# Two-layer hybrid block on one core: who adds the gated part to the residual in the last passes of the closing stages

## The chip, the cores and the metric

One of the cores of a Trainium2 chip runs the whole program; the other cores are idle. The metric is the time of one execution on the device in microseconds (us). Everything is float32; the matrix products are split by hand into a high and a low part and summed over three products. The engines are named as the profile names them: PE is TensorE, DVE VectorE, ACT ScalarE, POOL GpSimd, SP the engine that issues DMAs here.

## The reference, cut to what matters

Two layers. In each, a token-mixing sublayer and a feed-forward sublayer each end with the same three steps: an output product, a gated residual sum, and a layer norm over the 1024 channels.

```python
x = _layernorm(alpha * x + mod[2] * lat_mix, ln1_g[i], ln1_b[i])
x = _layernorm(alpha * x + mod[5] * _conv_ffn(_modulate(x, mod[3], mod[4]), lp), ln2_g[i], ln2_b[i])
if not last:
    xc = _layernorm(alpha * xc + mod_c[2] * ctx_mix, ln1_g[i], ln1_b[i])
    xc = _layernorm(alpha * xc + mod_c[5] * _conv_ffn(_modulate(xc, mod_c[3], mod_c[4]), lp), ln2_g[i], ln2_b[i])
```

`x` has 512 latent tokens and `xc` 256 context tokens, which are dropped after the first layer's updates. `alpha` is `ALPHA`, the fourth root of 4.

## The kernel before

The program is a row of stages. At the end of each, all engines meet at a barrier, so a stage is as long as the engine that ends last in it. Tokens lie on the 128 partitions: `x` is [128, tiles, 1024], with six tiles of tokens in the first layer (`nt` = 6) and four in the second (`nt` = 4). Two stages of each layer update `x`: `close` (from 1.3 to 1.49 ms in the first layer, and from 3.12 to 3.27 ms in the second) and `ffn` (after it, to 2.10 ms and to the end). This case is about the end of these four.

**The output product.** TensorE makes, for each tile t and each half n of the 1024 output channels, a 128x512 block in a PSUM bank. In `close` there are two passes over all tiles, c = 0 and c = 1; the last is written tile by tile (`project(1, t, ...)`) so that VectorE can follow. In `ffn` the hidden channels come in chunks, with passes (chunk, n); for the last chunk (`LC`) the order of the blocks is the list `final`: (0,0), (1,0), (0,1), (1,1), (2,0), (3,0), (2,1), (3,1), and so on, in pairs (t, n). A tile is complete when its block with n = 1 is.

**What VectorE does with a block** (`projected` in `close`, `gated` in `ffn`), one after the other:

- the gate: `part = PSUM block * gate row` (L2084, L2391), which signals `z1`. `part` has two buffers, taken in turn
- the add: `x = ALPHA * x + part` in the first passes (L2086), `x = x + part` in the later ones of `ffn` (L2397), which signals `z2`
- in the last passes, the statistics of this half, `bn_stats` (L2088, L2400)

When a tile is complete, `moments(t)`: aggregate (L2092, L2404), add epsilon (L2094, L2406), and `(x - mean) * ln_g` over 1024 columns (L2095, L2407). ScalarE takes the square root (`root`, L2046, L2358). Then `scaled(t)`: a reciprocal of one column (L2099, L2411) and `x * rstd + ln_b` over 1024 columns (L2102, L2414). Then `next_stats(t)`, except in the last `ffn`: two `bn_stats` of the new `x` for the next stage's norm (L2107, L2419). VectorE's order is the written one; a semaphore is waited for wherever the next instruction reads what another, its own too, has written.

**GpSimd** makes in these stages the low parts of the weights, 128x1024 each (L2055, L2367), and in `ffn` those of the hidden activations (L2375). It has nothing else in `close` and `ffn`, and is idle once the last weights are split. **ScalarE** makes the high parts (L2018, L2330) and then only the roots. **SP** loads the weights, and in the last `ffn` stores each tile of `x` when `scaled` is done with it.

Elsewhere, in attention, GpSimd squares what VectorE has copied (L1519). Its code is of use below, because one instruction in several has a second wait:

```python
if j >= 2:
    pool.wait_ge(sem("ss"), j - 1)
for u in range(nq):
    pool.wait_ge(sem("o_read"), j * nq + u + 1)
    o = oq[:, j * nq + u, :]
    m = pool.tensor_tensor(sq[:, j % 2, u, :], o, o, ALU.mult)
```

## Time and profile before

| what | value |
|---|---|
| time, median of 3 runs | 3673.91 us (3664.45 to 3676.2) |
| the profiled execution | 3661.34 us, of which its span is 3659.4 us |
| mean granted TensorE clock in it | 0.976 |
| TensorE busy | 3373.4 us, 92% |
| VectorE busy | 1584.3 us, 43% |
| ScalarE busy | 1268.5 us, 35% |
| GpSimd busy | 1074.0 us, 29% |

Over the whole program TensorE is the busiest engine by far. At the end of the four stages in question it is not: it has made its last block and stands still while VectorE finishes the tiles, and the next stage can't begin before. So what counts here is VectorE's own chain of instructions, from the timeline of these stretches, and not the shares of the whole span.

### The profile page before, as it was taken

What the parts mean: (1) busy time and instruction counts of PE and PEld (TensorE: products, weight loads), DVE (VectorE), ACT (ScalarE), POOL (GpSimd) and SP (SyncE); (2) the same over time, 40 slices, a digit from 0 to 9 for tenths busy, and PEclk for the clock granted to TensorE, in tenths of its full rate; (3) what the DMA queues carried; (4) which work ended last, traced back from release to release, by engine and by line L of the source; (5) the groups of instructions that cost most, each with busy time, mean ns of one, the idle gap of its engine ahead of it and who ended that gap; (6) DMA issues with size and microseconds to landing.
All of it is one profiled execution on the core that took longest, in us unless ns stands there. A gap on an engine that the chain in (4) does not pass through costs nothing. (4 is left out here: it accounts for less than half of the span.)

```text
span 3659.4 us, 82761 instructions
## 1 busy us (share of the span) xinstructions
PE 3373.4 (92%) x36725; PEld 2692.7 (74%) x36725; DVE 1584.3 (43%) x2538; ACT 1268.5 (35%) x2184; POOL 1074.0 (29%) x645
## 2 busy tenths in 40 slices
PE   6989999999888999799999899999999898879998
PEld 4668887888655777687878676887778666568887
DVE  3243335442277646612112734445453476372224
ACT  3333233333365422321212143334444365233222
POOL 1111132233011512233333232223333114235453
PEclk9999999999999999899999999999999999999999
DMA  7664332342222333233332145334443313423332
GB/s 264 209 203 113 109 111 87 114 130 83 78 72 76 120 124 125 74 122 116 115 121 93 34 154 177 106 110 126 123 129 90 104 58 121 164 85 104 98 98 87
DMA packets 444861, 423.43 MB, mean 116 GB/s; under 512 B 15652, under 2 KB 372042, under 8 KB 437594
## 3 DMA queue, kind: packets, MB, share of 16 engines
q1 hardware_dynamic: 442922, 409.35, 35.7%
q10 hardware_dynamic: 1584, 8.78, 0.6%
q8 instruction: 291, 4.77, 0.6%
q14 instruction: 64, 0.52, 0.0%
HBM read 329.34 MB, written 88.74 MB: 114 GB/s over the span
## 5 line engine op out<-in xcount | busy, mean ns | idle before, releaser
L888 PE MATMUL ps<-I-322_h_hi,I-325_w_hi 128*128 128x256 f32 (+1 forms) x832 | 297.3, 357 | 4.5 <-PEq L124 4.5
L888 PE MATMUL ps<-I-323_h_lo,I-325_w_hi 128*128 128x256 f32 (+1 forms) x832 | 281.9, 339 | 0.0
L888 PE MATMUL ps<-I-322_h_hi,I-326_w_lo 128*128 128x256 f32 (+1 forms) x832 | 281.4, 338 | 0.0
L2367 POOL TENSOR_TENSOR I-18801_w_lo<-I-18799_w_raw,I-18800_w_hi 128x1024 fp32r<-128x1024 f32 x60 | 144.9, 2415 | 343.5 <-ACT I-18800_w_hi L2330 343.4
L888 PE MATMUL ps<-I-23551_h_hi,I-23554_w_hi 128*128 128x512 f32 (+1 forms) x544 | 211.9, 389 | 4.6 <-PEq L124 4.6
L888 PE MATMUL ps<-I-23552_h_lo,I-23554_w_hi 128*128 128x512 f32 (+1 forms) x544 | 199.9, 368 | 0.0
L888 PE MATMUL ps<-I-23551_h_hi,I-23555_w_lo 128*128 128x512 f32 (+1 forms) x544 | 199.9, 367 | 0.0
L2367 POOL TENSOR_TENSOR I-39041_w_lo<-I-39039_w_raw,I-39040_w_hi 128x1024 fp32r<-128x1024 f32 x60 | 144.4, 2407 | 154.6 <-ACT I-39040_w_hi L2330 154.6
L2330 ACT ACTIVATE I-18800_w_hi<-I-18799_w_raw 128x1024 fp32r<-128x1024 f32 x61 | 64.6, 1060 | 355.6 <-PE ps L365 235.9
L365 PE MATMUL ps<-I-18796_h_hi,I-18800_w_hi 128*128 128x512 f32 x704 | 183.0, 341 | 1.1 <-DVE I-18797_h_lo L402 1.1
L365 PE MATMUL ps<-I-18796_h_hi,I-18801_w_lo 128*128 128x512 f32 x704 | 181.7, 339 | 0.0
L365 PE MATMUL ps<-I-18797_h_lo,I-18800_w_hi 128*128 128x512 f32 x704 | 181.6, 339 | 0.0
L852 POOL TENSOR_TENSOR I-326_w_lo<-I-324_w_raw,I-325_w_hi 128x1024 fp32r<-128x1024 f32 x34 | 83.1, 2443 | 326.2 <-ACT I-325_w_hi L1132 326.2
L888 PEld LDWEIGHTS ps<-I-322_h_hi,I-325_w_hi 128*128 128x128 f32 x832 | 158.2, 190 | 25.6 <-issue 4.9
L888 PEld LDWEIGHTS ps<-I-322_h_hi,I-326_w_lo 128*128 128x128 f32 x832 | 158.4, 190 | 17.4
L888 PEld LDWEIGHTS ps<-I-323_h_lo,I-325_w_hi 128*128 128x128 f32 x832 | 158.8, 191 | 13.9
L1114 ACT ACTIVATE I-2000_result<-ps 128x512 f32<-128x512 f32 x104 | 51.3, 493 | 329.4 <-PE ps L888 329.3
L852 POOL TENSOR_TENSOR I-23555_w_lo<-I-23553_w_raw,I-23554_w_hi 128x1024 fp32r<-128x1024 f32 x34 | 84.6, 2487 | 269.5 <-ACT I-23554_w_hi L1132 269.5
L958 PE MATMUL ps<-I-49_x 64*64 64x32 f32 x3840 | 148.7, 219 | 1.4 <-issue 0.9
L365 PE MATMUL ps<-I-39036_h_hi,I-39040_w_hi 128*128 128x512 f32 x352 | 137.5, 391 | 1.8 <-DVE I-39037_h_lo L402 1.8
L365 PE MATMUL ps<-I-39036_h_hi,I-39041_w_lo 128*128 128x512 f32 x352 | 137.0, 389 | 0.0
L365 PE MATMUL ps<-I-39037_h_lo,I-39040_w_hi 128*128 128x512 f32 x352 | 137.0, 389 | 0.0
(902 smaller groups left out, 8752.0 us busy)
## 6 DMA issues: line engine op xcount, KB each, us to landing
I-324_w_raw<-in_w_in SPq DMA_DIRECT2D x67, 512.0 KB, 5.9
I-23553_w_raw<-in_w_in SPq DMA_DIRECT2D x67, 512.0 KB, 5.2
I-18809_ada_w<-in_ada_w SPq DMA_DIRECT2D x24, 1024.0 KB, 6.0
I-18799_w_raw<-in_ffn_up SPq DMA_DIRECT2D x44, 512.0 KB, 3.9
I-39039_w_raw<-in_ffn_up SPq DMA_DIRECT2D x44, 512.0 KB, 3.9
proj_d<-I-2000_result SPq DMA_DIRECT2D x52, 384.0 KB, 3.1
I-508_ada_w<-in_ada_w SPq DMA_DIRECT2D x16, 1024.0 KB, 5.6
I-18799_w_raw<-in_ffn_down SPq DMA_DIRECT2D x22, 512.0 KB, 3.4
```

What stands on the lines that cost most here:

```text
L365: m = pe.matmul(dst[:, at:at + n], w[wi][:, k, :], a[ai][:, k, at:at + n], start=k == 0 and i == 0, stop=k == kt - 1 and i == 2)
L852: pool.tensor_tensor(lo(s), raw(s), hi(s).bitcast(F32), ALU.subtract).then_inc(sem("w_lo"), 1)
L888: m = pe.matmul(bank(6 + i % 2, n_c), w[:, k, :], hv[:, k, c0:c0 + n_c], start=k == 0 and v == 0, stop=k == KT - 1 and v == 2)
L958: return pe.matmul(side(ps[rows(i), (2 + d) * 512 + c0:(2 + d) * 512 + c0 + C], n_lv, 1 - d), Y[d][rows(i), c0:c0 + C], side(TT[d][rows(i) ...
L1114: act.activation(res[:, s % 2, c0:c0 + n_c], bank(6 + i % 2, n_c), ACT.Copy, scale=DH_A ** -0.5 if J_Q <= slots[s][0] < J_K else 1.0).then ...
L2330: act.activation(pair(g)[0], rings[0][:, g % 3, :, :], ACT.Copy).then_inc(sem("w_hi"), 1)
L2367: pool.tensor_tensor(pair(g)[1], rings[0][:, g % 3, :, :], pair(g)[0].bitcast(F32), ALU.subtract).then_inc(sem("w_lo"), 1)
```

## The change

In the last passes, all adds but the very last one of each stage move from VectorE to GpSimd. GpSimd gets a loop behind its weight splits: wait for the block's `z1` (the gate's product is in `part`), and for the add before it (`z2`), then `x = x + part` in place, signalling `z2`. In `close` that add had the factor `ALPHA` in it, which GpSimd's instruction doesn't; ScalarE multiplies the second half of every tile by `ALPHA` beforehand, in place, as soon as `x` is back in SBUF (semaphore `xa`).

VectorE's order in the last passes changes too. After the gate of block i it runs `scaled` and `next_stats` of the tile completed before (the "tile in front"), where there is one, and only then the statistics of block i, which need GpSimd's add; `moments` of the tile follows at once. The last tile's `scaled` and `next_stats` come behind the loop. In `close`, each block after the first has a tile in front. In `ffn`, a block has one only if the block before it in `final` has n = 1: (1,1), (2,0), (3,1) and (4,0) of twelve blocks in the first layer, (1,1) and (2,0) of eight in the second, beside the last block. The last block of a stage, whose add VectorE keeps, has one too.

```diff
--- before.py
+++ after.py
@@ -2045,6 +2045,9 @@
                         act.wait_ge(sem("var"), t + 1)
                         act.activation(rs[:, t:t + 1], rs[:, t:t + 1], ACT.Sqrt).then_inc(sem("std"), 1)
 
+                    act.wait_ge(sem("x_back"), 16)
+                    for t in range(nt):
+                        act.activation(x[:, t, 512:1024], x[:, t, 512:1024], ACT.Copy, scale=ALPHA).then_inc(sem("xa"), 1)
                     for t in range(nt):
                         root(t)
 
@@ -2054,6 +2057,12 @@
                         pool.wait_ge(sem("w_hi"), n - 1)
                         pool.tensor_tensor(lo(n)[:, 0:kt_of(n), :], raw(n)[:, 0:kt_of(n), :], hi(n)[:, 0:kt_of(n), :].bitcast(F32),
                                            ALU.subtract).then_inc(sem("w_lo"), 1)
+                    for t in range(nt - 1):
+                        i, xt = nt + t, x[:, t, 512:1024]
+                        pool.wait_ge(sem("xa"), t + 1)
+                        pool.wait_ge(sem("z1"), i + 1)
+                        pool.wait_ge(sem("z2"), i)
+                        pool.tensor_tensor(xt, xt, part[:, i % 2, :], ALU.add).then_inc(sem("z2"), 1)
 
                 @block.vector
                 def _(dve):
@@ -2082,8 +2091,19 @@
                         if i >= 2:
                             dve.wait_ge(sem("z2"), i - 1)
                         dve.tensor_tensor(part[:, i % 2, :], o_of(c, t), gate[:, t // LT, cols], ALU.mult).then_inc(sem("z1"), 1)
-                        dve.wait_ge(sem("z1"), i + 1)
-                        dve.scalar_tensor_tensor(x[:, t, cols], x[:, t, cols], ALPHA, part[:, i % 2, :], ALU.mult, ALU.add).then_inc(sem("z2"), 1)
+                        if c == 0 or t == nt - 1:
+                            dve.wait_ge(sem("z1"), i + 1)
+                            dve.wait_ge(sem("z2"), i)
+                            if c:
+                                dve.wait_ge(sem("xa"), nt)
+                                dve.tensor_tensor(x[:, t, cols], x[:, t, cols], part[:, i % 2, :], ALU.add).then_inc(sem("z2"), 1)
+                            else:
+                                dve.scalar_tensor_tensor(x[:, t, cols], x[:, t, cols], ALPHA, part[:, i % 2, :], ALU.mult, ALU.add).then_inc(sem("z2"), 1)
+                        if c == 0:
+                            moved(c, t)
+
+                    def moved(c, t):
+                        i, cols = c * nt + t, slice(c * 512, (c + 1) * 512)
                         dve.wait_ge(sem("z2"), i + 1)
                         dve.bn_stats(st[:, t, c, :], x[:, t, cols]).then_inc(sem("st"), 1)
 
@@ -2142,9 +2162,13 @@
                     dve.wait_ge(sem("ln_b"), 16)
                     for t in range(nt):
                         projected(1, t)
+                        if t:
+                            scaled(t - 1)
+                            next_stats(t - 1)
+                        moved(1, t)
                         moments(t)
-                        scaled(t)
-                        next_stats(t)
+                    scaled(nt - 1)
+                    next_stats(nt - 1)
 
         def ffn(l, h, last):
 
@@ -2374,6 +2398,11 @@
                             pool.wait_ge(sem("hf_hi"), j + 1)
                             pool.tensor_tensor(hp[1][:, j % CH, :], cv[:, j % 2, 0:n_tok], hp[0][:, j % CH, :].bitcast(F32),
                                                ALU.subtract).then_inc(sem("hf_lo"), 1)
+                    for t, n in final[:-1]:
+                        i, xt = 2 * LC * nt + final.index((t, n)), x[:, t, n * 512:(n + 1) * 512]
+                        pool.wait_ge(sem("z1"), i + 1)
+                        pool.wait_ge(sem("z2"), i)
+                        pool.tensor_tensor(xt, xt, part[:, i % 2, :], ALU.add).then_inc(sem("z2"), 1)
 
                 @block.vector
                 def _(dve):
@@ -2389,15 +2418,19 @@
                         if i >= 2:
                             dve.wait_ge(sem("z2"), i - 1)
                         dve.tensor_tensor(part[:, i % 2, :], pt_of(cn, t), gate[:, t // LT, c], ALU.mult).then_inc(sem("z1"), 1)
+                        if cn[0] == LC and (t, cn[1]) != final[-1]:
+                            return
                         dve.wait_ge(sem("z1"), i + 1)
+                        dve.wait_ge(sem("z2"), i)
                         if cn[0] == 0:
                             dve.scalar_tensor_tensor(x[:, t, c], x[:, t, c], ALPHA, part[:, i % 2, :], ALU.mult, ALU.add).then_inc(sem("z2"), 1)
                         else:
                             dve.wait_ge(sem("z2"), pass_no(cn) * nt + t + 1 - 2 * nt)
                             dve.tensor_tensor(x[:, t, c], x[:, t, c], part[:, i % 2, :], ALU.add).then_inc(sem("z2"), 1)
-                        if cn[0] == LC:
-                            dve.wait_ge(sem("z2"), i + 1)
-                            dve.bn_stats(st[:, t, cn[1], :], x[:, t, c]).then_inc(sem("st"), 1)
+
+                    def moved(t, n):
+                        dve.wait_ge(sem("z2"), 2 * LC * nt + final.index((t, n)) + 1)
+                        dve.bn_stats(st[:, t, n, :], x[:, t, n * 512:(n + 1) * 512]).then_inc(sem("st"), 1)
 
                     def moments(t):
                         dve.wait_ge(sem("st"), 4 * (t // 2) + 3 + t % 2)
@@ -2451,13 +2484,19 @@
                             ada_add(dve, sem, u, l + 1, u, 7)
                     dve.wait_ge(sem("ln_g"), 16)
                     dve.wait_ge(sem("ln_b"), 16)
-                    for t, n in final:
+                    def finished(t):
+                        scaled(t)
+                        if not last:
+                            next_stats(t)
+
+                    for i, (t, n) in enumerate(final):
                         gated((LC, n), t)
+                        if i and final[i - 1][1]:
+                            finished(final[i - 1][0])
+                        moved(t, n)
                         if n:
                             moments(t)
-                            scaled(t)
-                            if not last:
-                                next_stats(t)
+                    finished(final[-1][0])
 
         for l in range(DEPTH):
             last = l == DEPTH - 1
```

VectorE, `close` of the first layer, from `moments(0)` to `moments(1)`. Before:

```order
L2095 SCALAR_TENSOR_TENSOR I-49_x<-I-49_x,I-17270_mean_var,I-17267_ln_g 128x1024
L2099 RECIPROCAL I-17271_rstd<-I-17271_rstd 128x1
L2102 SCALAR_TENSOR_TENSOR I-49_x<-I-49_x,I-17271_rstd,I-17268_ln_b 128x1024
L2107 BN_STATS I-67_x_stats<-I-49_x 128x6 x2
L2084 TENSOR_TENSOR I-17265_part<-ps,I-17266_gate_row 128x512
L2086 SCALAR_TENSOR_TENSOR I-49_x<-I-49_x,I-17265_part 128x512
L2088 BN_STATS I-17269_stats<-I-49_x 128x6
L2092 BN_AGGR I-17270_mean_var<-I-17269_stats 128x2
L2094 TENSOR_SCALAR I-17271_rstd<-I-17270_mean_var 128x1
```

After:

```order
L2115 SCALAR_TENSOR_TENSOR I-49_x<-I-49_x,I-17270_mean_var,I-17267_ln_g 128x1024
L2093 TENSOR_TENSOR I-17265_part<-ps,I-17266_gate_row 128x512
L2119 RECIPROCAL I-17271_rstd<-I-17271_rstd 128x1
L2122 SCALAR_TENSOR_TENSOR I-49_x<-I-49_x,I-17271_rstd,I-17268_ln_b 128x1024
L2127 BN_STATS I-67_x_stats<-I-49_x 128x6 x2
L2108 BN_STATS I-17269_stats<-I-49_x 128x6
L2112 BN_AGGR I-17270_mean_var<-I-17269_stats 128x2
L2114 TENSOR_SCALAR I-17271_rstd<-I-17270_mean_var 128x1
```

The gate of tile 1 has moved in front of tile 0's reciprocal, and VectorE's add between the gate and the statistics is gone.

GpSimd, end of the first `close`, with the semaphores that each instruction waits for, in the order of the listing (a semaphore has the name of an earlier stage that had the same number: I-856 is `z2`, I-162 `z1` and I-247 `xa`). In the same listing the squares of attention (L1519) with two waits have `o_read` first and `ss` last. Before:

```order
L2055 TENSOR_TENSOR I-13893_w_lo<-I-13891_w_raw,I-13892_w_hi 128x512 [waits I-174_columns] x14
L2055 TENSOR_TENSOR I-13893_w_lo<-I-13891_w_raw,I-13892_w_hi 128x1024 [waits I-174_columns] x4
L2055 TENSOR_TENSOR I-17273_of_lo<-I-13891_w_raw,I-17272_of_hi 128x1024 [waits I-174_columns] x3
L2055 TENSOR_TENSOR I-13893_w_lo<-I-13891_w_raw,I-13892_w_hi 128x1024 [waits I-174_columns]
L119 UNCONDITIONAL_BRANCH
L123 ISA [waits barrier_Pool_Activation_PE_DVE_SP_gather]
```

After:

```order
L2058 TENSOR_TENSOR I-13893_w_lo<-I-13891_w_raw,I-13892_w_hi 128x512 [waits I-174_columns] x14
L2058 TENSOR_TENSOR I-13893_w_lo<-I-13891_w_raw,I-13892_w_hi 128x1024 [waits I-174_columns] x4
L2058 TENSOR_TENSOR I-17273_of_lo<-I-13891_w_raw,I-17272_of_hi 128x1024 [waits I-174_columns] x3
L2058 TENSOR_TENSOR I-13893_w_lo<-I-13891_w_raw,I-13892_w_hi 128x1024 [waits I-174_columns]
L2065 TENSOR_TENSOR I-49_x<-I-49_x,I-17265_part 128x512 [waits I-856_w_act,I-162_dots,I-247_ada_add] x5
L119 UNCONDITIONAL_BRANCH
L123 ISA [waits barrier_Pool_Activation_PE_DVE_SP_gather]
```

Behind the weight splits stand five adds, each with three waits, of which `z1` is the second. In `ffn` an add has two waits, listed as `z2` and then `z1`, which is last.

VectorE, last `ffn`, from the gate of block (2,0) to the gate of (2,1). Before:

```order
L2391 TENSOR_TENSOR I-39047_part<-ps,I-39048_gate_row 128x512
L2397 TENSOR_TENSOR I-49_x<-I-49_x,I-39047_part 128x512
L2400 BN_STATS I-39049_stats_out<-I-49_x 128x6
L2391 TENSOR_TENSOR I-39047_part<-ps,I-39048_gate_row 128x512
L2397 TENSOR_TENSOR I-49_x<-I-49_x,I-39047_part 128x512
L2400 BN_STATS I-39049_stats_out<-I-49_x 128x6
L2391 TENSOR_TENSOR I-39047_part<-ps,I-39048_gate_row 128x512
L2397 TENSOR_TENSOR I-49_x<-I-49_x,I-39047_part 128x512
L2400 BN_STATS I-39049_stats_out<-I-49_x 128x6
```

After:

```order
L2420 TENSOR_TENSOR I-39116_part<-ps,I-39117_gate_row 128x512
L2444 RECIPROCAL I-39120_rstd_out<-I-39120_rstd_out 128x1
L2447 SCALAR_TENSOR_TENSOR I-49_x<-I-49_x,I-39120_rstd_out,I-39122_ln_b 128x1024
L2433 BN_STATS I-39118_stats_out<-I-49_x 128x6
L2420 TENSOR_TENSOR I-39116_part<-ps,I-39117_gate_row 128x512
L2433 BN_STATS I-39118_stats_out<-I-49_x 128x6
L2420 TENSOR_TENSOR I-39116_part<-ps,I-39117_gate_row 128x512
L2433 BN_STATS I-39118_stats_out<-I-49_x 128x6
L2437 BN_AGGR I-39119_mean_var_out<-I-39118_stats_out 128x2
```

Tile 1's `scaled` stands between the gate and the statistics of (2,0); between gate and statistics of (3,0) there is nothing.

## Rows read from the trace of the kernel before

**Rows 1.** Stretches: from:to, us; busy PE, PEld, DVE, ACT, POOL; PEclk; DMA

```profile
1448.30:1486.80 38.50, 26.13 (x115) 21.12 (x113) 37.22 (x61) 1.22 (x6) 0.00 (x0) 0.87 0.00 0
2045.60:2100.30 54.70, 44.70 (x198) 36.68 (x196) 51.71 (x78) 3.56 (x8) 5.53 (x3) 0.95 0.02 7
```

**Rows 2.** Timeline (start, us, engine, line, operation, tiles): VectorE, a tile of close

```profile
1454.76 0.67 DVE L2084 TENSOR_TENSOR I-17265_part<-ps,I-17266_gate_row 128x512 f32<-128x512 f32 x1
1455.47 0.69 DVE L2086 SCALAR_TENSOR_TENSOR I-49_x<-I-49_x,I-17265_part 128x512 f32<-128x512 f32 x1
1456.19 0.69 DVE L2088 BATCH_NORM_STATS2 I-17269_stats<-I-49_x 128x6 f32<-128x512 f32 x1
...
1457.24 1.27 DVE L2095 SCALAR_TENSOR_TENSOR I-49_x<-I-49_x,I-17270_mean_var,I-17267_ln_g 128x1024 f32<-128x1024 f32 x1
1458.43 0.16 DVE L2099 RECIPROCAL I-17271_rstd<-I-17271_rstd 128x1 f32<-128x1 f32 x1
1458.62 1.28 DVE L2102 SCALAR_TENSOR_TENSOR I-49_x<-I-49_x,I-17271_rstd,I-17268_ln_b 128x1024 f32<-128x1024 f32 x1
1459.94 1.29 DVE L2107 BATCH_NORM_STATS2 I-67_x_stats<-I-49_x 128x6 f32<-128x512 f32 x2
1461.15 0.67 DVE L2084 TENSOR_TENSOR I-17265_part<-ps,I-17266_gate_row 128x512 f32<-128x512 f32 x1
```

**Rows 3.** Timeline: VectorE, end of the last ffn

```profile
3645.46 0.69 DVE L2391 TENSOR_TENSOR I-39047_part<-ps,I-39048_gate_row 128x512 f32<-128x512 f32 x1 [1.93 <-PE ps L2320]
...
3654.41 1.28 DVE L2414 SCALAR_TENSOR_TENSOR I-49_x<-I-49_x,I-39051_rstd_out,I-39053_ln_b 128x1024 f32<-128x1024 f32 x1
```

**Rows 4.** Timeline: GpSimd and VectorE at once, first passes of close in layer 1

```profile
3237.56 2.86 POOL L2055 TENSOR_TENSOR I-35367_w_lo<-I-35365_w_raw,I-35366_w_hi 128x1024 fp32r<-128x1024 f32 x1
...
3238.19 0.69 DVE L2088 BATCH_NORM_STATS2 I-37911_stats<-I-49_x 128x6 f32<-128x512 f32 x1
...
3241.67 2.39 POOL L2055 TENSOR_TENSOR I-35367_w_lo<-I-35365_w_raw,I-35366_w_hi 128x1024 fp32r<-128x1024 f32 x1 [1.25 <-ACT I-35366_w_hi L2018]
...
3242.32 2.29 DVE L2086 SCALAR_TENSOR_TENSOR I-49_x<-I-49_x,I-37907_part 128x512 f32<-128x512 f32 x1
```

**Rows 5.** Timeline: two pairs of GpSimd and VectorE that start almost together

```profile
1405.16 2.40 POOL L2055 TENSOR_TENSOR I-13893_w_lo<-I-13891_w_raw,I-13892_w_hi 128x1024 fp32r<-128x1024 f32 x1 [3.46 <-ACT I-13892_w_hi L2018]
...
1405.21 3.17 DVE L2124 TENSOR_TENSOR I-13890_y<-I-13890_y,I-17264_gated 128x768 f32<-128x768 f32 x1
...
2555.72 1.85 POOL L848 TENSOR_TENSOR I-23555_w_lo<-I-23553_w_raw,I-23554_w_hi 128x512 fp32r<-128x512 f32 x1 [6.95 <-ACT I-23554_w_hi L1130]
...
2555.74 0.69 DVE L1229 TENSOR_TENSOR I-24933_Bh<-I-24931_a,I-24929_EN 128x512 f32<-128x512 f32 x1
```

**Rows 6.** Timeline: VectorE releases GpSimd, at two places of attention

```profile
1002.35 0.29 DVE L1551 COPY I-49_x<-ps 128x128 f32<-128x128 f32 x1 [0.97 <-PE ps L1457]
...
1002.72 0.40 POOL L1519 TENSOR_TENSOR I-13908_o_sq<-I-49_x 128x128 f32<-128x128 f32 x1 [2.93 <-DVE I-49_x L1551]
...
1040.77 0.29 DVE L1551 COPY I-49_x<-ps 128x128 f32<-128x128 f32 x1 [0.61 <-PE ps L1457]
...
1041.21 0.40 POOL L1519 TENSOR_TENSOR I-13908_o_sq<-I-49_x 128x128 f32<-128x128 f32 x1 [4.07 <-DVE I-49_x L1551]
```

**Rows 7.** Line L864, ns min/median/max: in-place adds on GpSimd

```profile
L864 POOL TENSOR_TENSOR I-66_ada_row<-I-66_ada_row,I-2000_result x8: 1259/1288/1619, 477.9 to 897.3; 128x512 f32<-128x512 f32 x8
```

**Rows 8.** Timeline: the first ffn as its last chunk opens, GpSimd and VectorE

```profile
2048.28 2.85 POOL L2367 TENSOR_TENSOR I-18797_h_lo<-I-18799_w_raw,I-18796_h_hi 128x1024 fp32r<-128x1024 f32 x1
...
2055.07 0.69 DVE L2400 BATCH_NORM_STATS2 I-18810_stats_out<-I-49_x 128x6 f32<-128x512 f32 x1
```

**Rows 9.** Timeline: ScalarE around the last passes of the first close

```profile
1441.60 1.06 ACT L2018 ACTIVATE I-13892_w_hi<-I-13891_w_raw 128x1024 fp32r<-128x1024 f32 x1 [8.86 <-PE ps L1962]
1442.67 1.28 ACT L2046 ACT_TABLE_LOAD   x1
...
1450.96 0.20 ACT L2046 ACTIVATE I-17271_rstd<-I-17271_rstd 128x1 f32<-128x1 f32 x1 [7.01 <-DVE I-17271_rstd L2094]
```

## The prediction

> **What bounds the kernel now.** I read the table of stretches first, for the ends of the four stages [rows 1]. In the last passes of the first `close` VectorE is busy for 37.22 of 38.50 us and in those of the first `ffn` for 51.71 of 54.70, TensorE for 26.13 and 44.70: TensorE is ahead, and the stage ends with VectorE. Then the timeline of VectorE [rows 2]. One tile of `close` takes from 1454.76 to 1461.15, 6.39 us, with no gap longer than a semaphore. The last `ffn` is the exception: before the gate of (2,1) VectorE waits 1.93 us for TensorE [rows 3]. What is lost before that point costs only what exceeds 1.93; from there on all of it counts, since the last `x * rstd + ln_b` ends at 3655.69 and its store closes the program. So the change is worth what it does to VectorE's chain, four times, and it hangs on three things: what an add costs on GpSimd, whether something covers it, and which engine gets in first where both want to read two SBUF tiles.
>
> **Two engines at once.** [rows 4] and [rows 5] show what overlap does. VectorE's add at 3242.32 takes 2.29 us, not 0.69, and ends 0.55 after GpSimd's split (3244.61 against 3244.06): it had to wait for the whole GpSimd instruction and lost 0.14 less than its length. The statistics at 3238.19, with one SBUF input, take 0.69 with GpSimd at work. So gates (one input in PSUM) and statistics run beside a GpSimd add; `(x - mean) * ln_g` and `x * rstd + ln_b` do not. The other way round GpSimd waits: at 2555.74 VectorE has its 0.69 us although it starts 0.02 after GpSimd, whose split takes 1.85 and ends 1.14 after VectorE's end. At 1405.21, 0.05 behind GpSimd, VectorE waits (3.17 us). The border lies between 0.02 and 0.05 us.
>
> **An add that nothing covers.** GpSimd's in-place add of 128x512 takes 1.29 us in the median, 1.26 to 1.62 [rows 7]; I take 1.29. The handover from VectorE to GpSimd takes 0.08 us with one wait (1002.64 to 1002.72) and 0.15 where the late semaphore is listed before another (1041.06 to 1041.21) [rows 6]. The adds of `ffn` have `z1` last, so 0.08; those of `close` have it in the middle, so 0.15. Back to VectorE I take 0.07. From the gate's end to the statistics are now 0.08 + 1.29 + 0.07 = 1.44 us in `ffn` and 1.51 in `close`; before, 1456.19 - 1455.43 = 0.76 [rows 2]. A bare add costs **0.68** or **0.75 us**.
>
> **An add with a tile in front.** Let the gate end at T. The reciprocal starts 0.08 before T and `x * rstd + ln_b` 0.19 after that, at T + 0.11 (as 1458.51, 1458.43 and 1458.62 in [rows 2]).
> In `close` GpSimd comes at T + 0.15, after VectorE: VectorE runs to T + 1.39, GpSimd ends 1.14 later, at T + 2.53, and the two statistics for the next stage run meanwhile, to T + 2.72. The block's own statistics start at T + 2.64, when the add has just landed (2.60): nothing is lost. The tile is shorter by the add (0.72) and by 0.12, since the reciprocal no longer waits behind a dependent instruction: **-0.84 us**, 5.55 for 6.39.
> In `ffn` GpSimd comes at T + 0.08, 0.03 to 0.04 before VectorE. That is inside the border of [rows 5]; it is nearer to the 0.05 that lost, so I let GpSimd win. It ends at T + 1.37 and VectorE 1.28 - 0.14 = 1.14 later, at T + 2.51 for T + 1.39. The 1.12 us are more than the 0.84: **+0.28 us**.
>
> What a blocked GpSimd add costs after VectorE's end is 1.14 here. The Trainium skill (SBUF — State Buffer, "A bandwidth-pool intuition that's wrong (but worth ruling out)") gives for descriptor work of GpSimd "blocked until DVE-end + ~115 ns". By it the add would end at T + 2.80, 0.27 later than by the row, the statistics would wait about 0.23, and the six covered tiles of `close` would make the sum 1.4 us larger; I go by the row.
>
> **The four stages.**
> - First `close`: adds of tiles 0 to 4 moved, tile 0 bare, four covered; tile 5 keeps its add but gains the 0.12: 0.75 - 4 x 0.84 - 0.12 = **-2.7**.
> - Second `close`: 0.75 - 2 x 0.84 - 0.12 = **-1.1**.
> - First `ffn`. At its opening GpSimd still splits weights. The last split, 2.85 us from 2048.28 [rows 8], is 0.45 shorter once VectorE no longer cuts in: it ends at 2050.68, and only then comes the add of (0,0), which on VectorE slipped in between two splits. Add to 2051.97, statistics 2052.04, gate of (1,0) 0.61 later, to 2053.33, statistics 2054.77, gate of (0,1) to 2056.06, statistics 2057.50, where they were at 2055.07: +2.4. Then four covered (+1.1), four bare ((3,0), (2,1), (5,0), (4,1): +2.7), and -0.12: **+6.1**.
> - Last `ffn`: the same opening +2.4, covered (1,1) and (2,0) +0.6, bare (3,0) +0.7, together 3.7, of which 1.93 go into the wait for TensorE [rows 3]: +1.8. Bare (2,1) +0.7, -0.1: between 2.1 and 2.4, **+2.2**.
>
> ScalarE's six multiplications by `ALPHA` cost nothing: 128x1024 takes it 1.06 us and it is idle for 7.01 from 1443.95 on [rows 9]; even at 1.06 each they and the table load end by 1450.4, before the first root at 1450.96, and the first, wanted at 1449.1, by 1443.8. Without that cover the first GpSimd add would wait. VectorE's additional waits on `z2` are met before they are asked. TensorE's banks are freed by the gates, which in `close` come earlier; in the first `ffn` they come up to 2 us later, and TensorE is several us ahead. VectorE has nothing queued behind the new wait for GpSimd that could run meanwhile, which is why a bare add costs its full length.
>
> The sum is -2.7 - 1.1 + 6.1 + 2.2 = **+4.5 us**, on a profiled execution of 3661.34 (span 3659.4): 3665.8. That execution lies 12.6 below the median, 3673.91, so against the median I say **3678.4**.
>
> **Rivals.**
> - GpSimd first everywhere. The order in `close` rests on a difference of 0.04 us. For it: the handover in `close` is taken from one place with two waits, not three. Against: [rows 6] has the same listing. Then each of the six covered tiles costs +0.28 and not -0.84, and a bare one 0.68: +1.7 and +1.1 for the two `close`, in all +11.1, 3685.0.
> The Trainium skill (SBUF — State Buffer, "Who interferes with whom") has it that "Issue order, not op shape, decides who blocks"; that rule gives either outcome.
> - VectorE first everywhere, as the 0.02 of [rows 5] allows. The covered blocks of the first `ffn` then gain 0.84: +1.6. In the last there are no statistics for a next stage to cover the rest of the add (T + 2.60 against T + 2.43), so it becomes +2.6. In all +0.4 to +1, 3674.6.
> - The slower one: GpSimd's add is long. [rows 7] has 1.62 beside 1.29. If that is its price on `x`, and GpSimd goes first, all 26 adds (5 + 3 + 11 + 7) stand in VectorE's chain with 0.33 more each: 11.1 + 8.6 = +19.7, 3693.6. With GpSimd first, any add over 1.29 carries the sum over 11 us, which is 0.3%. Against: the median of eight is 1.288, and the maximum looks like one that waited for VectorE.
> - The faster one: no lock between these instructions. The covered blocks gain everywhere, and the sum is about -2, 3672. Against it stand [rows 4, 5].
>
> **How the numbers follow.** The forecast has 0.47, VectorE first 0.22, GpSimd first 0.19, the long add 0.08, no lock 0.04. A measurement of this kernel can tell about 0.3%, 11 us, from no change. Of the forecast and its neighbours nearly all lies within it; of GpSimd first about half, since 11.1 is on the border. Slower by over 0.3%: 0.08 + 0.09 = 0.17. Faster by over 0.3% comes from no case, only from the spread of runs: 0.04. Within: 0.79. For the range I add to the cases the spread of the runs, 3664.45 to 3676.2: 3664 to 3688 leaves out the long add and little else.
>
> **What would show it.** Right: in `close`, tiles 1 to 4 at 5.55 us each, `x * rstd + ln_b` at 1.28 us, GpSimd adds recorded as about 2.4 us because they wait; in `ffn`, `x * rstd + ln_b` of covered blocks at about 2.4 us beside GpSimd adds of 1.29; bare blocks with 1.4 to 1.5 us from the gate's end to the statistics; the first `ffn` some 6 us longer, the last 2. Wrong: the durations exchanged between the two engines; bare adds well over 1.3; GpSimd's first add of `ffn` not behind the splits; or another part of the program that moves by more than the four ends, as the TensorE clock after them could.

## The result, and the profile of the changed kernel

The changed kernel takes **3682.17 us** (median of 13 executions, 3673.85 to 3689.55), the kernel before 3670.26 (13, 3664.45 to 3676.2). The ratio is **1.0034**, with a 95% interval from 1.0024 to 1.0043: slower by 12.5 us (8.8 to 15.8). The profiled execution of the changed kernel has a span of 3677.2 us. Of the experiments below, e5 had two executions out of eleven that took 4281 and 4287 us at a granted clock of 0.74; they are left out of its ratio.

Most of what follows is measured by four **ends**: from the first gate of the last passes to the first aggregate of the next stage's norm, and in the last `ffn` to the end of the span. The kernel before has 39.43, 55.59, 26.58 and 38.27 us in program order. The changed kernel has 41.32, 61.01, 27.69 and 40.08: +1.89, +5.42, +1.11, +1.81, together **+10.24 us**. The two spans differ by 17.8; 7.0 of that are there before the first changed place (its gate is at 1455.37 for 1448.37), where the two programs do the same work. Executions of one kernel differ by as much, so I go by the ends, and for the whole by the ratio.

The profile of the changed kernel, its head and then the two stretches that answer to [rows 1] (from:to, us; busy PE, PEld, DVE, ACT, POOL; PEclk; DMA):

```profile
span 3677.2 us, 82811 instructions
...
PE 3381.7 (92%) x36725; PEld 2699.5 (73%) x36725; DVE 1572.0 (43%) x2512; ACT 1272.8 (35%) x2194; POOL 1105.7 (30%) x671
```

```profile
1455.30:1495.50 40.20, 26.11 (x115) 21.10 (x113) 37.75 (x56) 1.22 (x6) 6.45 (x5) 0.85 0.00 0
2052.40:2112.20 59.80, 44.71 (x198) 36.69 (x196) 44.92 (x67) 3.56 (x8) 19.13 (x14) 0.91 0.02 6
```

In the first `close` VectorE has five instructions less, but its busy time has not fallen (37.75 for 37.22): what remains takes longer. In the first `ffn` it is busy 6.8 us less than before, in a stretch that is 5.1 longer: it stands idle.

VectorE, first `close`, from the gate of tile 0 to that of tile 2, as in [rows 2] (start, us, engine, line, operation, tiles):

```profile
1455.37 0.67 DVE L2093 TENSOR_TENSOR I-17265_part<-ps,I-17266_gate_row 128x512 f32<-128x512 f32 x1
1457.50 0.69 DVE L2108 BATCH_NORM_STATS2 I-17269_stats<-I-49_x 128x6 f32<-128x512 f32 x1 [1.46 <-POOL I-49_x L2065]
...
1459.74 0.68 DVE L2093 TENSOR_TENSOR I-17265_part<-ps,I-17266_gate_row 128x512 f32<-128x512 f32 x1
1460.34 0.15 DVE L2119 RECIPROCAL I-17271_rstd<-I-17271_rstd 128x1 f32<-128x1 f32 x1
1460.53 2.41 DVE L2122 SCALAR_TENSOR_TENSOR I-49_x<-I-49_x,I-17271_rstd,I-17268_ln_b 128x1024 f32<-128x1024 f32 x1
1462.97 1.29 DVE L2127 BATCH_NORM_STATS2 I-67_x_stats<-I-49_x 128x6 f32<-128x512 f32 x2
1464.17 0.68 DVE L2108 BATCH_NORM_STATS2 I-17269_stats<-I-49_x 128x6 f32<-128x512 f32 x1
...
1466.39 0.69 DVE L2093 TENSOR_TENSOR I-17265_part<-ps,I-17266_gate_row 128x512 f32<-128x512 f32 x1
```

GpSimd in the same stretch:

```profile
1456.18 1.29 POOL L2065 TENSOR_TENSOR I-49_x<-I-49_x,I-17265_part 128x512 f32<-128x512 f32 x1 [4.05 <-DVE I-17265_part L2093]
1460.56 1.30 POOL L2065 TENSOR_TENSOR I-49_x<-I-49_x,I-17265_part 128x512 f32<-128x512 f32 x1 [3.09 <-DVE I-17265_part L2093]
```

`x * rstd + ln_b` takes 2.41 us for the 1.28 of [rows 2], and GpSimd's add has its 1.30: GpSimd holds the way to SBUF and VectorE waits, although the record has GpSimd start 0.03 us *behind* VectorE. A tile takes 6.65 us (1459.74 to 1466.39) where it took 6.39. All four covered adds of the first `close` and both of the second read like this.

The first `ffn`: VectorE in the opening, with the statistics of (0,0) and the gate and statistics of (0,1), and `x * rstd + ln_b` under the first covered add, that of (1,1); then GpSimd in the same stretch:

```profile
2058.76 0.69 DVE L2433 BATCH_NORM_STATS2 I-18836_stats_out<-I-49_x 128x6 f32<-128x512 f32 x1 [5.62 <-POOL I-49_x L2405]
...
2062.05 0.67 DVE L2420 TENSOR_TENSOR I-18833_part<-ps,I-18834_gate_row 128x512 f32<-128x512 f32 x1
2064.12 0.69 DVE L2433 BATCH_NORM_STATS2 I-18836_stats_out<-I-49_x 128x6 f32<-128x512 f32 x1 [1.40 <-POOL I-49_x L2405]
...
2067.14 2.33 DVE L2447 SCALAR_TENSOR_TENSOR I-49_x<-I-49_x,I-18838_rstd_out,I-18840_ln_b 128x1024 f32<-128x1024 f32 x1
```

```profile
2049.40 8.08 POOL L2391 TENSOR_TENSOR I-18823_h_lo<-I-18825_w_raw,I-18822_h_hi 128x1024 fp32r<-128x1024 f32 x3
2057.45 1.28 POOL L2405 TENSOR_TENSOR I-49_x<-I-49_x,I-18833_part 128x512 f32<-128x512 f32 x1
...
2062.80 1.28 POOL L2405 TENSOR_TENSOR I-49_x<-I-49_x,I-18833_part 128x512 f32<-128x512 f32 x1 [1.40 <-DVE I-18833_part L2420]
2067.11 1.28 POOL L2405 TENSOR_TENSOR I-49_x<-I-49_x,I-18833_part 128x512 f32<-128x512 f32 x1 [3.03 <-DVE I-18833_part L2420]
```

Here GpSimd starts 0.03 ahead and wins, as forecast. The first add begins only behind the third weight split, so that VectorE waits 5.62 us, and a bare add keeps it idle for 1.40 us.

### The profile page after: what moved, and what is told of

Its sections match the earlier page's. It is cut to its first block and busy times, and to the rows that moved or that the text cites. A ratio compares the mean times of both kernels' runs of the same rounds, so it can differ in the third digit from the quotient of the medians.

```text
span 3677.2 us, 82811 instructions
## 1 busy us (share of the span) xinstructions
PE 3381.7 (92%) x36725; PEld 2699.5 (73%) x36725; DVE 1572.0 (43%) x2512; ACT 1272.8 (35%) x2194; POOL 1105.7 (30%) x671
## 5 line engine op out<-in xcount | busy, mean ns | idle before, releaser
L2391 POOL TENSOR_TENSOR I-18827_w_lo<-I-18825_w_raw,I-18826_w_hi 128x1024 fp32r<-128x1024 f32 x60 | 145.2, 2421 | 342.2 <-ACT I-18826_w_hi L2354 342.0
L888 PE MATMUL ps<-I-23602_h_hi,I-23605_w_hi 128*128 128x512 f32 (+1 forms) x544 | 212.2, 390 | 4.6 <-PEq L124 4.6
L888 PE MATMUL ps<-I-23603_h_lo,I-23605_w_hi 128*128 128x512 f32 (+1 forms) x544 | 200.2, 368 | 0.0
L888 PE MATMUL ps<-I-23602_h_hi,I-23606_w_lo 128*128 128x512 f32 (+1 forms) x544 | 200.2, 368 | 0.0
L2391 POOL TENSOR_TENSOR I-39110_w_lo<-I-39108_w_raw,I-39109_w_hi 128x1024 fp32r<-128x1024 f32 x60 | 144.3, 2406 | 154.8 <-ACT I-39109_w_hi L2354 154.8
L365 PE MATMUL ps<-I-18822_h_hi,I-18826_w_hi 128*128 128x512 f32 x704 | 183.0, 341 | 1.1 <-DVE I-18823_h_lo L402 1.1
L365 PE MATMUL ps<-I-18822_h_hi,I-18827_w_lo 128*128 128x512 f32 x704 | 182.0, 340 | 0.0
L365 PE MATMUL ps<-I-18823_h_lo,I-18826_w_hi 128*128 128x512 f32 x704 | 180.0, 337 | 0.0
L888 PEld LDWEIGHTS ps<-I-322_h_hi,I-326_w_lo 128*128 128x128 f32 x832 | 159.3, 191 | 17.8
L365 PE MATMUL ps<-I-39105_h_hi,I-39109_w_hi 128*128 128x512 f32 x352 | 137.6, 391 | 1.8 <-DVE I-39106_h_lo L402 1.8
L365 PE MATMUL ps<-I-39105_h_hi,I-39110_w_lo 128*128 128x512 f32 x352 | 137.0, 389 | 0.0
```

The source lines that it names most:

```text
L365: m = pe.matmul(dst[:, at:at + n], w[wi][:, k, :], a[ai][:, k, at:at + n], start=k == 0 and i == 0, stop=k == kt - 1 and i == 2)
L888: m = pe.matmul(bank(6 + i % 2, n_c), w[:, k, :], hv[:, k, c0:c0 + n_c], start=k == 0 and v == 0, stop=k == KT - 1 and v == 2)
L2391: pool.tensor_tensor(pair(g)[1], rings[0][:, g % 3, :, :], pair(g)[0].bitcast(F32), ALU.subtract).then_inc(sem("w_lo"), 1)
```

## The experiments

| kernel | four ends, against before | sum | ratio to before (95%) |
|---|---|---|---|
| changed kernel | +1.89, +5.42, +1.11, +1.81 | +10.24 | 1.0034 (1.0024 to 1.0043) |
| e1_vector_first | -2.56, +1.27, -1.13, +2.22 | -0.21 | 0.9999 (0.9987 to 1.0012) |
| e2_close_alone | +1.89, +0.01, +1.12, +0.02 | +3.05 | 1.0015 (1.0006 to 1.0025) |
| e3_order_alone | -0.17, -0.24, +0.17, +0.30 | +0.06 | 1.0004 (0.9994 to 1.0014) |
| e4_covered_vector_first | -3.12, -0.81, -1.45, +0.30 | -5.08 | 0.9983 (0.9973 to 0.9992) |
| e5_last_block_old_order | -3.12, -1.07, -1.44, 0.00 | -5.64 | 0.9980 (0.9970 to 0.9991) |
| e6_one_wait_more | -2.59, +5.66, -1.15, +1.88 | +3.80 | 1.0006 (0.9995 to 1.0018) |
| e7_opening_back | +1.88, +3.88, +1.11, +0.51 | +7.38 | not timed |
| e8_two_waits_more | -2.57, +1.27, -0.84, +2.17 | +0.03 | 0.9997 (0.9986 to 1.0008) |
| e9_e5_again | -3.13, -1.09, -1.46, -0.01 | -5.69 | 0.9979 (0.9967 to 0.9990) |

Each ratio is against executions of the kernel before on the same occasion. The ratios follow the sums: times 3670, they are +12.5, -0.4, +5.5, +1.5, -6.2, -7.3, +2.2, -1.1 and -7.7 us, and the interval of each holds its sum.

**e1: GpSimd made to come second.** Each covered add also waits for the reciprocal of the tile in front, behind which VectorE's `x * rstd + ln_b` stands.

```diff
+                        if t:
+                            pool.wait_ge(sem("rstd"), t)
...
+                        e = final.index((t, n))
+                        if e and final[e - 1][1]:
+                            pool.wait_ge(sem("rstd"), final[e - 1][0] + 1)
```

> The changed kernel, but every GpSimd add that has a tile in front also waits for the reciprocal of that tile, so that it starts some 0.1 us after VectorE's x * rstd + ln_b instead of within 0.04 us of it. Theory (the loss in the covered blocks is the shared read path, taken by the engine that asks first, and GpSimd asked first in both stages): VectorE's x * rstd + ln_b goes from about 2.4 us back to 1.28, the GpSimd adds are recorded at about 2.3, a tile of close takes 5.55 us for 6.64 of the changed kernel, the covered blocks of the first ffn 1.1 us less each. The four ends together: +0.6 us against the kernel before, where the changed kernel had +10.2; ratio about 1.000. Rival (GpSimd has precedence whoever asks first, or the slow x * rstd + ln_b has another reason): the instruction stays at 2.4 us, each covered tile gets another 0.1 us longer, the ends stay at +10 to +11.

VectorE's and GpSimd's rows of the first covered pair:

```profile
1460.91 1.28 DVE L2124 SCALAR_TENSOR_TENSOR I-49_x<-I-49_x,I-17271_rstd,I-17268_ln_b 128x1024 f32<-128x1024 f32 x1
```

```profile
1461.05 2.30 POOL L2067 TENSOR_TENSOR I-49_x<-I-49_x,I-17265_part 128x512 f32<-128x512 f32 x1 [3.20 <-DVE I-17271_rstd L2121]
```

The durations have changed engines: 1.28 and 2.30. The tile of `close` takes 5.53 us, for the 5.55 that I had worked out for this order. The order of the two engines at twelve places is worth 10.4 us, as much as the whole slowdown. Against the numbers of the rival "VectorE first everywhere", the two `ffn` come to +1.27 and +2.22 for +1.6 and +2.6.

**e2: the change in `close` alone**, both `ffn` as before.

```diff
-                    for t, n in final[:-1]:
-                        i, xt = 2 * LC * nt + final.index((t, n)), x[:, t, n * 512:(n + 1) * 512]
-                        pool.wait_ge(sem("z1"), i + 1)
-                        pool.wait_ge(sem("z2"), i)
-                        pool.tensor_tensor(xt, xt, part[:, i % 2, :], ALU.add).then_inc(sem("z2"), 1)
...
-                            finished(final[i - 1][0])
```

> Only the two close stages are changed, both ffn are those of the kernel before. Theory (the loss is made of bare adds and of lost races, block by block): the closes keep +1.9 and +1.1 us, the ffn stages are as before, together +3.0 us, ratio 1.001. Rival (the changed kernel's time comes mainly from outside the four ends, where its profiled execution was 7 us later before the first of them began): the ratio stays at 1.002 or more though the ffn stages are as before.

The ends add: the stages do not act on each other. TensorE's clock in the stretches behind them, which the prediction named as a possible second effect, doesn't show in them: the unchanged stages stay within 0.02 us.

**e3: VectorE's new order alone.** All adds stay on VectorE; it finishes the tile in front behind the next gate, and makes the add and the statistics after that. In `moved` of both stages stands (here that of `ffn`)

```diff
+                        dve.wait_ge(sem("z1"), i + 1)
+                        dve.tensor_tensor(x[:, t, c], x[:, t, c], part[:, i % 2, :], ALU.add).then_inc(sem("z2"), 1)
```

(in `close` the add is the one with `ALPHA`, as before), and GpSimd's loops and ScalarE's multiplications are gone.

> VectorE's new order (gate of the next block, then reciprocal, x * rstd + ln_b and statistics of the tile in front, then the block's own add and statistics) with all adds still on VectorE; nothing on GpSimd, no multiplication on ScalarE. Theory: the order gains 0.12 us for each block with a tile in front, since two dependent instructions no longer stand next to each other, 16 blocks in all: the ends together -1.6 to -1.9 us; nothing waits for GpSimd, x * rstd + ln_b takes 1.28 us everywhere. Rival (the order itself costs something, as through ScalarE's root coming late or stores going out late): the ends at or above zero.

This missed. A tile of `close` does gain 0.12 (6.27 for 6.39), but VectorE now asks for the gate before it finishes the tile in front, and may have to wait for a bank that TensorE hasn't filled, in `close` and in the first `ffn`:

```profile
1458.78 0.69 DVE L2084 TENSOR_TENSOR I-17265_part<-ps,I-17266_gate_row 128x512 f32<-128x512 f32 x1 [0.39 <-PE ps L1962]
...
2062.02 0.69 DVE L2400 TENSOR_TENSOR I-18807_part<-ps,I-18808_gate_row 128x512 f32<-128x512 f32 x1 [0.31 <-PE ps L2329]
```

Before, the work on the tile in front filled these waits. In the last `ffn` the gain falls into waits for TensorE, and what the old order had done there now stands behind the last gate.

**e4: only covered adds on GpSimd, and VectorE first.** As e1, but VectorE keeps the add of tile 0 in `close`, the eight uncovered blocks of the first `ffn`, and all of the last `ffn`.

```diff
-                    for t in range(nt - 1):
+                    for t in range(1, nt - 1):
...
+            given = [] if last else [b for a, b in zip(final, final[1:]) if a[1] and b != final[-1]]
-                    for t, n in final[:-1]:
+                    for t, n in given:
```

> Only the adds that have a tile in front and next-stage statistics to hide under are on GpSimd (four in the first close, two in the second, four in the first ffn, none in the last), with the wait for the reciprocal as in e1; the bare ones are back on VectorE. Theory: -0.84 us for each of the ten and -0.12 for the last block of each stage: -3.5, -1.8, -3.5 and -0.1, together -8.9 us, ratio 0.9976, faster than both kernels. Rival (precedence of GpSimd): +0.3 us for each of the ten, together +3 us, ratio 1.001.

The two `close` come 0.4 us short of what was expected (-3.12 for -3.5, -1.45 for -1.8): the gate of tile 1 waits 0.40 and 0.30 us for TensorE there, as in e3. The first `ffn` is far short: -0.81 for -3.5. There the eleven intervals from gate to gate add up to 44.7 us, 4.06 each, and four of them are 4.08, which is what TensorE takes for a block. So TensorE sets the pace of the gates now, and VectorE waits for it:

```profile
2087.27 0.69 DVE L2426 TENSOR_TENSOR I-18837_part<-ps,I-18838_gate_row 128x512 f32<-128x512 f32 x1 [0.66 <-PE ps L2347]
...
2091.35 0.69 DVE L2426 TENSOR_TENSOR I-18837_part<-ps,I-18838_gate_row 128x512 f32<-128x512 f32 x1 [0.31 <-PE ps L2347]
...
2092.88 1.28 DVE L2453 SCALAR_TENSOR_TENSOR I-49_x<-I-49_x,I-18842_rstd_out,I-18844_ln_b 128x1024 f32<-128x1024 f32 x1
2094.19 1.29 DVE L2458 BATCH_NORM_STATS2 I-67_x_stats<-I-49_x 128x6 f32<-128x512 f32 x2
```

Before the gates of this stretch VectorE waits 3.45 us for TensorE in all, where it waited 1.22 before: 2.2 of the missing 2.7 us. The last gate comes 3.4 us earlier against the first than before (44.7 for 48.1), but tile 4's last two steps now stand behind it, and the rest of the stage is 10.08 us long for 7.47.

**e5: the old order where GpSimd has no add.** As e4, but VectorE finishes the tile in front ahead of the gate for the last block of the first `ffn` and in all of the last `ffn`.

```diff
                     for i, (t, n) in enumerate(final):
+                        if i and final[i - 1][1] and (t, n) not in given:
+                            finished(final[i - 1][0])
                         gated((LC, n), t)
-                        if i and final[i - 1][1]:
+                        if i and final[i - 1][1] and (t, n) in given:
                             finished(final[i - 1][0])
```

> As e4_covered_vector_first, with one edit: VectorE finishes the tile in front (scaled, and next_stats where there is one) before the gate, as the kernel before does, for the last block of the first ffn and for all blocks of the last ffn; only where GpSimd has the add (the two close stages, and the covered blocks of the first ffn) it is finished behind the gate. Theory A (e4's shortfall in the first ffn is that TensorE's blocks, 4.08 us apart, set its gates, so that work put behind the last gate, which comes when TensorE has made its block, only makes the tail longer): the first ffn improves from -0.81 to about -1.1, the last ffn from +0.30 to 0.0, the two close stay at -3.1 and -1.45; sum -5.7 for e4's -5.08. Theory B (the shortfall is a cost of the GpSimd add in these blocks, not of the order): both ffn stages stay as in e4, sum -5.1. Against the kernel before the ratio would be about 0.998 by either.

As by the first theory: -1.07 and 0.00. The order at these blocks is worth 0.26 and 0.30 us. The rest of e4's shortfall stays, as do the intervals between the gates up to the last but one, and VectorE still waits 3.18 us for TensorE: it is TensorE's pace, with 44.7 us of work in a stretch that was 48.1.

**e9: e5 once more.**

> The kernel of e5_last_block_old_order once more on another occasion, because two of its eleven executions took 4281 and 4287 us at a mean granted clock of 0.74, with nothing else unusual. Theory A (a disturbance from outside the kernel): no such execution here, ends of the four stages as in e5 within 0.1 us (-3.1, -1.1, -1.4, 0.0), ratio to the kernel before between 0.997 and 0.999. Theory B (the kernel's order of work brings the clock down now and then): about one execution in five again over 4200 us at a clock of about 0.74.

None of its twelve executions took more than 3675.29 us, which speaks for theory A; what disturbed the two isn't known. The ends repeat within 0.02 us. This kernel is **faster than the kernel before**, by 0.2%, and so than the changed one, whose ratio is 1.0034.

**e6 and e8: waits that order nothing.** Each covered GpSimd add of the changed kernel gets one more wait (e6), in `ffn` a second one (e8), for things made microseconds earlier.

```diff
+                        if t:
+                            pool.wait_ge(sem("mv"), t)
...
+                        e = final.index((t, n))
+                        if e and final[e - 1][1]:
+                            pool.wait_ge(sem("mv"), final[e - 1][0] + 1)
+                            pool.wait_ge(sem("st"), 4 * (final[e - 1][0] // 2) + 3 + final[e - 1][0] % 2)
```

The last line is e8's alone.

> The changed kernel with one more wait in front of each covered GpSimd add, on the aggregate of the tile in front, which is made some microseconds earlier, so that the wait is met before it is asked. It orders nothing; it can only make GpSimd's instruction start a few hundredths of a microsecond later. Theory A (whoever starts first by some border holds both engines' way to SBUF; in the changed kernel GpSimd starts 0.033 us behind VectorE in close and still wins, the border is 0.033 to 0.044): in close the GpSimd add starts 0.05 to 0.1 later, VectorE wins, tiles go from 6.64 to 5.53 and the two close stages from +1.9 and +1.1 to about -2.6 and -1.1; in ffn GpSimd starts at most 0.04 behind VectorE and still wins, tiles stay at 6.58, +5.4 and +1.8; sum about +3.5. If the additional wait costs more there (0.06 or more behind VectorE), ffn's covered tiles go to 5.53 too and the sum is about -0.2. Theory B (what e1 changed was the order given by the added dependence and its length of over 0.1 us, and a few hundredths decide nothing): tiles stay at 6.64 and 6.58, sum +10.2.

> As e6_one_wait_more, with a second wait that is met before it is asked (on the statistics of the tile in front) before each covered GpSimd add of the two ffn stages; in the listing z1, the late one, then stands first with three behind it, as in close in e6, where that put GpSimd's start 0.124 to 0.131 us behind VectorE's. Theory A (whoever starts first holds the way to SBUF, and waits listed behind the late one delay the start by about 0.05 us each): in ffn too GpSimd starts 0.12 to 0.13 behind VectorE and VectorE wins; covered tiles go from 6.64 to 5.53; the four ends are those of e1_vector_first, -2.6, +1.3, -1.1 and +2.2, sum -0.2 against the kernel before and -10.4 against the changed kernel; the ratio to before is 1.000, where the changed kernel's was 1.0034. Theory B (in ffn e1's dependence on the reciprocal was needed, a mere delay isn't enough): ffn stays as in e6, +5.7 and +1.9, sum +3.8, ratio 1.001.

e6, VectorE and then GpSimd, a covered pair of the first `close` and one of the first `ffn`:

```profile
1458.74 1.28 DVE L2124 SCALAR_TENSOR_TENSOR I-49_x<-I-49_x,I-17271_rstd,I-17268_ln_b 128x1024 f32<-128x1024 f32 x1
...
2061.63 2.40 DVE L2452 SCALAR_TENSOR_TENSOR I-49_x<-I-49_x,I-18842_rstd_out,I-18844_ln_b 128x1024 f32<-128x1024 f32 x1
```

```profile
1458.87 2.30 POOL L2067 TENSOR_TENSOR I-49_x<-I-49_x,I-17265_part 128x512 f32<-128x512 f32 x1 [3.19 <-DVE I-17265_part L2095]
...
2061.66 1.29 POOL L2410 TENSOR_TENSOR I-49_x<-I-49_x,I-18837_part 128x512 f32<-128x512 f32 x1 [3.09 <-DVE I-18837_part L2425]
```

e8, the same pair of `ffn`:

```profile
2063.45 1.29 DVE L2453 SCALAR_TENSOR_TENSOR I-49_x<-I-49_x,I-18842_rstd_out,I-18844_ln_b 128x1024 f32<-128x1024 f32 x1
```

```profile
2063.57 2.32 POOL L2411 TENSOR_TENSOR I-49_x<-I-49_x,I-18837_part 128x512 f32<-128x512 f32 x1 [3.19 <-DVE I-18837_part L2426]
```

In `close` the one wait puts GpSimd's start from 0.03 to 0.13 us behind VectorE's, and VectorE wins: 5.53 us for a tile. In `ffn` it puts it from 0.03 ahead to 0.03 behind, and GpSimd still wins; with the second it is 0.13 behind and VectorE wins. A delay of GpSimd by 0.10 to 0.15 us at twelve places takes 10.2 us off the changed kernel. The end of e8's second `close` is 0.3 us short of the forecast: VectorE stands 1.24 us at the barrier there, where it is 0.95 in e6.

**e7: the opening of `ffn` on VectorE again**, the adds of (0,0) and (1,0).

```diff
-                    for t, n in final[:-1]:
+                    for t, n in final[2:-1]:
...
-                        if cn[0] == LC and (t, cn[1]) != final[-1]:
+                        if cn[0] == LC and (t, cn[1]) in final[2:-1]:
```

> The changed kernel with the adds of the first two blocks of each ffn's last passes, (0,0) and (1,0), on VectorE again; GpSimd's adds begin with (0,1). Theory A (the opening costs about 2.2 us in the first ffn because GpSimd's first add waits behind its last weight split, and then two adds stand bare): the first ffn goes from +5.4 to about +3.9 (two bare adds at 0.68 gone, and the wait for the split gone or hidden), the last ffn from +1.8 to about +0.5; the close stages stay at +1.9 and +1.1; sum about +7.4. Theory B (the opening's loss is a wait of VectorE for TensorE or weights that the adds have nothing to do with): the sum stays at +10.2.

As expected, +3.88 and +0.51. These two adds cost the changed kernel 1.54 us in the first `ffn` and 1.30 in the last. What is left of the +2.2 at the statistics of (0,1) is 0.7, the bare add of that block.

## Why the prediction was right in its range and wrong in its mechanism

The predicted time, 3678.4 us, is 3.8 below what was measured, and the range holds it. The difference to the kernel before was forecast as +4.5; it is +10.2 by the ends and +12.5 by the ratio, just over the 0.3% that the forecast took as the bound of "same". That is the rival "GpSimd first everywhere", +11.1, to which I gave 0.19. The miss lies in the two `close`: +1.9 and +1.1 where -2.7 and -1.1 were forecast; the two `ffn` came 0.7 and 0.4 below their forecast. The time fits better than the difference by luck: the median of three runs that it starts from, 3673.91, lies 3.65 above that of the thirteen, 3670.26.

- **The step that failed** is "In `close` GpSimd comes at T + 0.15, after VectorE: VectorE runs". It takes 0.04 us behind VectorE for a safe distance, because the border had been read from [rows 5] as "between 0.02 and 0.05 us" with GpSimd ahead. In all six covered tiles of `close` GpSimd was recorded 0.027 to 0.035 us behind, and it won. The 0.02 of [rows 5] isn't a start against an idle engine. The instruction in front of it, in the trace of before:

```profile
2555.13 0.68 DVE L1227 TENSOR_TENSOR I-24943_kk_in<-I-24943_kk_in,I-24937_Lx 128x512 f32<-128x512 f32 x1
```

  also reads two SBUF tiles, and VectorE follows straight on. And the same pair stands in every trace of this case. In the changed kernel's, 0.02 us apart as well, it comes out the other way:

```profile
2566.64 1.29 POOL L848 TENSOR_TENSOR I-23606_w_lo<-I-23604_w_raw,I-23605_w_hi 128x512 fp32r<-128x512 f32 x1 [6.95 <-ACT I-23605_w_hi L1130]
```

```profile
2566.66 1.81 DVE L1229 TENSOR_TENSOR I-24984_Bh<-I-24982_a,I-24980_EN 128x512 f32<-128x512 f32 x1
```

  VectorE waits there and in seven other traces; it wins in before, e7 and e9. So 0.02 ahead was itself the border, and one for a VectorE that follows straight on. Where VectorE has finished what stood in front of it, and that read PSUM or one SBUF tile, as in the covered tiles, the border is another, and the trace of before has pairs on its far side that the prediction didn't use. Here VectorE is 0.05 ahead, with the gate's input in PSUM in front of it, and wins:

```profile
3126.13 0.69 DVE L2124 TENSOR_TENSOR I-35364_y<-I-35364_y,I-37906_gated 128x512 f32<-128x512 f32 x1
...
3126.18 1.78 POOL L2055 TENSOR_TENSOR I-35367_w_lo<-I-35365_w_raw,I-35366_w_hi 128x512 fp32r<-128x512 f32 x1 [9.50 <-ACT I-35366_w_hi L2018]
```

  Before has eight such pairs, with GpSimd 0.044 to 0.052 behind, all like this. Over the eleven traces, GpSimd won 25 of 26 such pairs when it was recorded 0.018 to 0.035 behind (the one that it lost is in e4, at 0.032) and none of 89 at 0.038 to 0.056. So by recorded starts this border lies between 0.03 and 0.04 us behind VectorE.
- **The starts were right to 0.01 us**, and that 0.01 counted: GpSimd at T + 0.14 (forecast 0.15) and VectorE at T + 0.11 in `close`; T + 0.08 and T + 0.11 in `ffn`. At the 0.04 that the forecast had in `close`, VectorE would probably have won after all; the rows of before couldn't decide it, and the rival said that the order rests on this difference. What each order costs was right as well: a tile of `close` takes 5.53 with VectorE first (5.55), 6.65 with GpSimd first (6.39 + 0.28). The first `close` came out at 0.70 (the bare tile) + 4 x 0.255 - 0.12 + 0.29, where 0.29 is the barrier: VectorE stands there for 1.31 us, for 1.02 before. The prediction has no term for it. The second is 0.70 + 2 x 0.27 - 0.12.
- **Bare adds**: 0.70 us in `close` (0.75 forecast), 0.64 in `ffn` (0.68; 2.68 for 2.04 from gate to gate). The 1.29 of [rows 7] is right, so the long add falls.
- **Covered adds of `ffn`**: +0.19 (6.58 for 6.39), forecast +0.28. The forecast let VectorE end 1.14 after GpSimd's end; it is 1.08.
- **The opening**: +2.2 (the statistics of (0,1) at 2064.12, 11.7 us after the first gate), forecast 2.4. Thus the first `ffn` is 2.2 + 4 x 0.64 + 4 x 0.19 - 0.12 = 5.4 for 6.1, and the last 1.81 for 2.2.
- **ScalarE's multiplications** cost nothing, as forecast: six in 3.22 us from 1449.54, and the root's table is loaded by 1454.05, 4.61 us before the first root.

Of the two rules of the Trainium skill in the prediction, "Issue order, not op shape, decides who blocks" (SBUF — State Buffer, "Who interferes with whom") leaves out that GpSimd may be recorded up to 0.035 us later and still be the one that blocks. The other, "blocked until DVE-end + ~115 ns" (the Trainium skill, the same page, "A bandwidth-pool intuition that's wrong (but worth ruling out)"), which is measured there on descriptor work, is not what an add shows: the whole of it ends 1.15 us after VectorE, which is 0.14 less than its own 1.29.

## What to carry to other kernels

When work moves to an engine that shares a way to memory with the first, work out which of the two comes first at that moment, and make the order certain by a dependence rather than by some hundredths of a microsecond: here that decided between +10 and 0 us. Move only what something covers (a bare add lost 0.64 to 0.70 us each time), and keep the work on the tile in front ahead of a wait that may be long, since behind it the wait is idle. And ask how far the other engine is behind: where TensorE had 44.7 us of work in 48.1, four covered adds gained 1.1 us and not 3.5.

## What the runs showed of the hardware

- Where both engines read two SBUF tiles and VectorE has finished what stood in front (which read PSUM or one SBUF tile), GpSimd wins also when it is recorded 0.026 to 0.035 us later (the covered pairs of `close` in the changed kernel, e2 and e7 and of `ffn` in e6, 24 in all); it lost one pair at 0.032 (e4), one at 0.038 (e2), eight at 0.044 to 0.052 (before), and all covered pairs at 0.124 to 0.140 (e1, e4, e5, e8, e9 and the `close` of e6).
- Where VectorE follows straight on another instruction that reads two SBUF tiles, the border is elsewhere: with GpSimd recorded 0.019 to 0.022 us ahead, VectorE won in three traces and waited in eight. That the instruction in front shifts the border is my reading; no run changes it alone.
- The one that loses waits for the whole of the other's instruction. VectorE's 1.29 us end 1.08 after GpSimd's end, GpSimd's 1.29 us end 1.15 after VectorE's: the loser is 1.0 to 1.1 us longer either way, so it matters which of them is on the path.
- Further waits of one instruction that are already met aren't free: each one listed behind the late one puts GpSimd's start back by about 0.05 us. Against VectorE's start it went from 0.026 ahead to 0.028 and 0.126 behind with none, one and three in `ffn`, and from 0.03 to 0.128 behind with one and three in `close`. A wait listed before the late one shows no such cost: the adds of `ffn`, with two waits and the late one last, start 0.08 behind the gate's end, as the squares of attention do with one [rows 6]. No run changes only the order of the same waits.
- At the barrier behind the first `close` VectorE stands for 1.31 us in the changed kernel, e1, e2, e6, e7 and e8, for 1.02 in before and e3, and for 0.95 in e4, e5 and e9. The profile names TensorE's sequencer, which is only the last to go on. In the changed kernel VectorE's own signal (L119) comes 0.4 us after its drain has ended, and 0.05 us after it in before; what holds it back is open.
